# Earlier expert loads into reordered slots, a shorter router gap, and token rows gathered by DMA for experts 1 to 7

## The reference

```
def moe_swiglu(v, router, wg, wu, wd):
    logits = (v @ router).astype(F32)
    top_val, top_idx = lax.top_k(logits, TOP_K_EXPERTS)       # 2 of 8
    top_w = jax.nn.softmax(top_val, axis=-1)
    combine = jnp.sum(jax.nn.one_hot(top_idx, N_EXPERTS, dtype=F32) * top_w[..., None], axis=-2)
    ...
    for e in range(N_EXPERTS):
        y = y + combine[..., e:e + 1] * swiglu(v, wg[e], wu[e], wd[e])
    return y
```

## Time and profile before

| | us |
|---|---|
| median of 3 executions | 1486.5 (1485.67 to 1486.66) |
| profiled execution, its own time | 1487.51 |
| its span in the profile | 1485.8 |
| PE busy | 1453.5 (98%) |
| DVE, ACT, POOL busy | 619.3, 458.5, 39.9 |

### The profile page before, as it was taken

How to read it: one execution, slowest core, us unless ns; L and a number is a source line. 1 busy time by engine, 2 the same in 40 slices (tenths; PEclk the granted TensorE clock), 3 DMA queues, 4 the chain that set the end, 5 groups by cost and what they waited for, 6 DMA issues and landing times.

```text
span 1485.8 us, 28756 instructions
## 1 busy us (share of the span) xinstructions
PE 1453.5 (98%) x12424; PEld 1015.2 (68%) x12424; DVE 619.3 (42%) x879; ACT 458.5 (31%) x653; POOL 39.9 (3%) x73
## 2 busy tenths in 40 slices
PE   8999999999999999999999999999999999999967
PEld 7888788888888888888886743576346733576226
DVE  5877797645455677788840010101000010101024
ACT  5656444534445555653420000000000000000024
POOL 3200000000000010000000000000000000000000
PEclk9999999999999999999999999999999999999999
DMA  8355455556656544545669999999999999999980
GB/s 300 126 169 170 143 160 168 188 180 195 196 174 197 165 143 141 172 143 180 241 268 405 408 405 407 408 405 408 406 408 406 407 405 402 408 401 408 401 329 29
DMA packets 160948, 411.35 MB, mean 277 GB/s; under 512 B 16386, under 2 KB 41780, under 8 KB 160820
## 3 DMA queue, kind: packets, MB, share of 16 engines
q1 hardware_dynamic: 159168, 407.69, 74.1%
q10 hardware_dynamic: 1652, 1.80, 0.4%
HBM read 408.38 MB, written 1.05 MB: 276 GB/s over the span
## 4 chain that ended last, share of the span: by engine, by line
PE 92%; DMA 3%; SPq 2%; DVE 1%; issue 1%; ACT 0%; POOL 0%; POOLq 0%; DVEq 0%; ACTq 0%
PE ps L2044 35%; PE ps L1594 15%; PE ps L1596 15%; PE ps L1595 15%; SPq L532 2%; PE ps L2013 2%; PE ps L2036 1%; PE ps L1693 1%; DMA arena<-in_moe_wd 1%; DMA expert_ring<-in_moe_wd 1%; DMA split_area_hi<-in_moe_wd 1%; PE ps L1654 1%; PE ps L1840 1%; PE ps L1703 1%; PE ps L1864 1%
## 5 line engine op out<-in xcount | busy, mean ns | idle before, releaser
L1594 PE MATMUL ps<-whi,ahi 128*128 128x512 f32 (+1 forms) x984 | 391.7, 398 | 4.5 <-DVE wlo L994 2.3
L1596 PE MATMUL ps<-wlo,ahi 128*128 128x512 f32 (+1 forms) x984 | 383.7, 390 | 0.0
L1595 PE MATMUL ps<-whi,alo 128*128 128x512 f32 (+1 forms) x984 | 383.0, 389 | 0.0
L994 DVE TENSOR_TENSOR wlo<-arena,whi 128x1024 fp32r<-128x1024 f32 (+1 forms) x246 | 289.0, 1217 | 91.4 <-ACT whi L649 90.4
L649 ACT ACTIVATE whi<-arena 128x1024 fp32r<-128x1024 f32 (+1 forms) x246 | 245.7, 1053 | 97.1 <-PE ps L1596 89.2
L2044 PE MATMUL ps<-arena 128*32 128x512 f32 (+3 forms) x2724 | 224.8, 471 | 8.3 <-DMA arena<-in_moe_wu 8.3
L1594 PEld LDWEIGHTS ps<-whi,ahi 128*128 128x128 f32 x984 | 185.1, 188 | 47.4 <-issue 9.0
L1596 PEld LDWEIGHTS ps<-wlo,ahi 128*128 128x128 f32 x984 | 184.9, 188 | 39.0
L1595 PEld LDWEIGHTS ps<-whi,alo 128*128 128x128 f32 x984 | 185.4, 188 | 35.6
L2044 PEld LDWEIGHTS ps<-arena 128*32 128x32 f32 x2724 | 115.7, 110 | 103.2 <-issue 57.9
L1511 DVE TENSOR_TENSOR ff_area<-ff_area,ps 128x768 f32<-128x768 f32 (+1 forms) x24 | 19.7, 821 | 388.4 <-PE ps L2044 388.4
(11 more groups left out here) (263 smaller groups left out, 1014.8 us busy)
## 6 DMA issues: line engine op xcount, KB each, us to landing
arena<-in_w_in SPq DMA_DIRECT2D x112, 512.0 KB, 4.5
arena<-in_moe_wd SPq DMA_DIRECT2D x92, 512.0 KB, 12.5
arena<-in_moe_wu SPq DMA_DIRECT2D x78, 512.0 KB, 13.3
arena<-in_moe_wg SPq DMA_DIRECT2D x68, 512.0 KB, 13.6
expert_ring<-in_moe_wd SPq DMA_DIRECT2D x52, 512.0 KB, 12.3
expert_ring<-in_moe_wg SPq DMA_DIRECT2D x46, 512.0 KB, 13.3
expert_ring<-in_moe_wu SPq DMA_DIRECT2D x34, 512.0 KB, 14.4
arena<-in_moe_wg SPq DMA_DIRECT2D x42, 384.0 KB, 12.5
```

What stands on the lines that cost most here:

```text
L994: return V.tensor_tensor(dst, src, hi.bitcast(f32), ALU.subtract)
L1594: TE.matmul(o, ahi[:, sa], whi[:, sw], start=start, stop=False)
L1595: TE.matmul(o, alo[:, sa], whi[:, sw], start=False, stop=False)
L1596: return TE.matmul(o, ahi[:, sa], wlo[:, sw], start=False, stop=stop)
```

## The change

The diff has three parts.

1. **Slots.** The place `turned_v` in `EXTRA`, which waited for the router, becomes `states`: the same columns of `arena`, but free once a mixer step is done (`pe_step`), since the turned activations (`VT`) move to other columns. `FREED` is reordered, each slot waits for its own last user (slots 5 and 6 wait for `acc_out_dve` and `merged_ready`, not for `aT_ready`), and granules 0 and 1 of the experts are issued between the loads of `w_out` (`EARLY`).
2. **Router gap.** The second row of throw-away transposes has 3 in place of 16. The tokens of expert 0 are gathered by 16 float32 products from `u_nat`, as those of the others were, in place of 32 split ones. The low parts on DVE are gone.
3. **Rows.** POOL stores the normed activations to a DRAM buffer of 1 MB. For each of experts 1 to 7 PE works out which token is in which slot (two products with one column, `tokens_of_slots`), DVE casts that to integers, POOL issues an indirect DMA that gathers 64 or 96 rows of 4 KB into `wk(YM, ...)`, and PE transposes them (`turn_rows`, 4 transposes for each half) in place of the 8 products for each half.

```
-EXTRA = ("keys", "split_hi", "split_lo", "turned_v")
+EXTRA = ("keys", "states", "split_hi", "split_lo")
...
-FREED = [FIRST_EXTRA + i for i in range(3)] + [4, 5, 6]
-for last in range(M0 - RAW, M0):
-    FREED += [last % RAW] + (pair_of(last % WR) if last >= M0 - WR else [])
-FREED.insert(8, FIRST_EXTRA + 3)
+FREED = [FIRST_EXTRA + i for i in range(len(EXTRA))] + [5, 6, 4]
+FREED += [last % RAW for last in range(M0 - RAW, M0)]
+for last in range(M0 - WR, M0):
+    FREED += pair_of(last % WR)
+EARLY = {M0 - 4: 0, M0 - 3: 1}
...
+            def gather_rows():
+                for t in range(NT):
+                    pool.wait_ge(v_nat, t + 1)
+                    pool.dma_start(v_dram[t * P:(t + 1) * P, :], u_nat(t)).then_inc(v_stored, 16)
+                pool.wait_ge(v_stored, 16 * NT)
+                for e in range(1, NE):
+                    pool.wait_ge(slots_ready, e)
+                    if e > 1:
+                        pool.wait_ge(combined, NT * (e - 1))
+                    pool.indirect_dma_start(out=wk(YM, D)[0:CAPS[e]], out_offset=None, in_=v_dram[:, :],
+                                            in_offset=bass.IndirectOffsetOnAxis(ap=token_of[0:CAPS[e], e:e + 1], axis=0))\
+                        .then_inc(tokens_landed, 16)
...
                             if kind == "down" and j == 3:
+                                if e + 1 < NE:
+                                    dve.wait_ge(slots_done, e + 1)
+                                    V.tensor_copy(token_of[:, e + 1:e + 2], bank(7, 1, 500)).then_inc(slots_ready, 1)
...
-                    keep_busy(16, 0)
+                    keep_busy(3, 0)
...
+                    def tokens_of_slots():
+                        for t in range(NT):
+                            last = TE.matmul(bank(7, 1, 500), psel[:, t * P:(t + 1) * P].bitcast(f32), token_ids[:, t:t + 1],
+                                             start=t == 0, stop=t == NT - 1)
+                        last.then_inc(slots_done, 1)
+                    def turn_rows(e, half):
+                        n = CAPS[e]
+                        for c in range(4):
+                            last = TE.transpose(bank(7, n, c * n), wk(YM + (4 * half + c) * P, P)[0:n], ident[0:n, 0:n])
+                        last.then_inc(gathered, 1)
...
                             if j in (6, 7) and e + 1 < NE:
                                 if j == 6:
-                                    pe.wait_ge(onehot, 2 * e + 4)
+                                    pe.wait_ge(tokens_landed, 16 * (e + 1))
                                     pe.wait_ge(turned_out, e + 1)
...
-                                gather_rank(e + 1, j - 6)
+                                turn_rows(e + 1, j - 6)
```

More of the change, by code:

```diff
@@ L152, in raw @@
                     return arena[:, T + 1024:T + 1024 + GRAN]
-                if where == "turned_v":
+                if where == "states":
                     return arena[:, T + 3072:T + 3072 + GRAN]
@@ L487, in split, with fetch @@
                 sp.wait_ge(lo_ready, 2 * (n + 1))
+            of_place = [0]
+            def fetch(m):
+                slot = SLOT_OF[m]
+                if BEFORE[m] is not None:
+                    sp.wait_ge(gemm_done, M0 + BEFORE[m] + 1)
+                elif slot >= FIRST_EXTRA:
+                    if EXTRA[slot - FIRST_EXTRA] == "keys":
+                        sp.wait_ge(hg_x, 8 * DEPTH)
+                    elif EXTRA[slot - FIRST_EXTRA] == "states":
+                        sp.wait_ge(pe_step, N_STEPS + 32)
+                    else:
+                        sp.wait_ge(gemm_done, L1 + G_BR + 4)
+                elif slot >= ARENA_SLOTS:
+                    ring = (slot - ARENA_SLOTS) % WR
+                    sp.wait_ge(gemm_done, max(n for n in range(M0) if n % WR == ring) + 1)
+                elif slot < RAW:
+                    split(max(n for n in range(M0) if n % RAW == slot))
+                elif slot == 4:
+                    sp.wait_ge(at_ready, 4 * 6)
+                elif slot == 5:
+                    sp.wait_ge(acc_out_dve, upto(DVE_OUT, 1, A_BR + 4))
+                else:
+                    sp.wait_ge(merged_ready, 4)
+                for src, how, w in moe_granule(of_place[m // PER_E], m % PER_E) if m < N_MOE else granule(1, G_PLE0 + m - N_MOE):
+                    sp.dma_start(place(slot, how, w), src).then_inc(moe_landed[slot], 16)
             for n in range(M0):
@@ L513, in _ @@
                     of_place += [sp.value_load(order[0:1, RANK[e]:RANK[e] + 1], min_val=0, max_val=NE - 1) for e in range(1, NE)]
[L514 to L532, removed]
+                fetch(m)
             sp.wait_ge(gemm_done, M0 + N_MOE)
@@ L2117, in transpose_ff @@
                         last.then_inc(m_tr, 1)
-                    pe.wait_ge(v_lo, NT)
+                    pe.wait_ge(v_nat, NT)
+                    pe.wait_ge(onehot, 2)
                     for half in range(2):
-                        gather(half, onehot, 2, gathered)
+                        gather_rank(0, half, 6 + half)
                     for e in range(NE):
@@ L2153, in _ @@
                                 transpose_ff(e, PAIRS - 1, j - 6)
+                            if j == 2 and e + 1 < NE:
+                                pe.wait_ge(onehot, 2 * e + 4)
+                                if e > 0:
+                                    pe.wait_ge(slots_ready, e)
+                                tokens_of_slots()
                             if j == 4:
```

69 lines of the change are left out of this document (32 added, 37 removed).

## The result

The changed kernel takes 1497.8 us (median of 1494.3, 1497.8 and 1498.7) against 1486.5; the ratio is 1.0066, with a 95% interval of 1.0053 to 1.0080. That ratio makes 9.8 us (7.9 to 11.9) of the 1486.5, where +1.4 was forecast, and outside the range of 1481.5 to 1493. It is not the quotient of the two medians, which lie 11.3 us apart; in all that follows, differences of time go by such ratios. The profiled execution took 1494.3 us with a span of 1492.5, so the trace is that of the fastest of the three. The kernel is still one stream of DMAs with a tail, and most rows look as forecast. As in the rows of before, a row of windows has the stretch and its length, then busy us (instructions) of PE, PEld, DVE, ACT and POOL, the granted clock of PE, the share of the DMA engines, and GB/s.

The account below looks back on a forecast made before the run. One stream of expert-weight DMAs at full rate plus a 44.5 us tail bounds the kernel. Profiled 1487.5 us, -3.4 for lead, +4.8 for rows, gives 1488.9; the median is 1.0 lower: 1487.9 us, range 1481.5 to 1493.

Parts of the forecast that it names:

- What bounds the kernel: From 762 us on: one stream of weight DMAs at full rate, then a tail of 44.5 us the change leaves alone.
- The slots: Before the experts: no pause at 750 to 762 us, 17 granules issued by 757 us, slots full at about 768.
- PE's start: Behind the router: gather starts 2.5 us earlier at about 765.6 and, slowed 1.45 us by the clock, ends 1.05 earlier.
- slower by the clock: Rival: PE at 1.2 GHz through gather and first granule, experts start 1.5 us later; 1491.4 us, chance 0.10.
- The lead at granule 34: In expert 0: old backlog of 5.8 us plus 0.5 from PE's earlier start, so the stream is 6.3 us ahead.
- The pause at the table reads: At 822 to 828 us: SP's seven reads leave the engines dry for 5.5 - 2.58 = 2.9 us.
- The lead kept: Behind the table reads: 6.3 - 2.9 = 3.4 us, kept to the end.
- PE's 14.5 us: In experts 1 to 7: PE work saved by transposes in place of gather products, worth nothing at the end.
- The rows: In the experts' stream: 480 gathered rows of 4 KB, 1.97 MB, priced by bytes at 4.8 us.
- The upper bound, 9.7: High bound in us for the cost of the gathered rows: twice their bytes.
- slower by the rows: Rival: rows fetched singly through POOL's descriptors cost twice their bytes, 9.7 us; 1492.8 us, chance 0.14.
- The gathers were never late: In experts 1 to 7: rows asked for 17 us ahead in the shortest case; PE's waiting for them costed at nothing.

Follow-up runs that it names:

- e1: The change's slots and router gap only, tokens of experts 1 to 7 gathered by PE products as before, no indirect DMAs; 1483.2 us, ratio 0.9979.
- e9: Changed kernel with a plain DMA of 64 rows on POOL's queue, onto every second partition, for each indirect one; 1489.1 us, ratio 1.0010.
- e11: The change's slots and router gap, all gathers on PE, SP's table reads moved ahead of granule 17; 1485.1 us, ratio 0.9980.
- e13: Changed kernel with a plain DMA of 64 rows on POOL's queue, onto partitions 0 to 63, for each indirect one; 1493.8 us, ratio 1.0036.
- e2: Changed kernel without its seven indirect DMAs, turning and other waits kept, wrong tokens for experts 1 to 7; 1483.7 us, ratio 0.9985.
- e12: Changed kernel with only SP's table reads moved ahead of granule 17; 1494.2 us, ratio 1.0043.
- e14: Changed kernel without its indirect DMAs and with SP's table reads moved ahead of granule 17; 1482.1 us, ratio 0.9968.
- e4: The changed kernel measured again, nothing altered; 1495.3 us, ratio 1.0067.
- e7: Changed kernel with a plain DMA of the first 64 or 96 rows on POOL's queue for each indirect one; 1495.0 us, ratio 1.0049.
- e8: Changed kernel with a plain DMA of 64 or 96 rows on ACT's hardware queue for each indirect one; 1496.4 us, ratio 1.0055.

## Why the prediction was wrong, step by step

- **What bounds the kernel: right.** One stream, an end set by its last landing, a tail of 43.9 us (44.5 before).
- **The slots: right.** No pause at 750 to 762 us, 17 granules issued by 756.1 us (757), dry at 770 (768). The two early granules held nothing back.
- **PE's start: right in size (first product 2.7 us earlier, 1.2 without the offset, forecast 1.05), with the clock's loss in another place.** The forecast had the lower level last until 768.5 and slow the gather by 1.45 us. In this trace it lasted as long (6.8 us) but from 757.8 to 764.6, and fell on the second half of the router's products and the 14 transposes. First before, then after:

```profile
759.02 1.95 PE L1976 MATMUL ps<-router,arena 128*128 128x8 f32 x16 [0.61 <-ACT arena L855]
```
```profile
757.52 3.35 PE L2008 MATMUL ps<-router,arena 128*128 128x8 f32 x16 [0.61 <-ACT arena L890]
758.00:762.00 4.00, 4.00 (x20) 4.00 (x20) 0.92 (x8) 2.69 (x4) 1.72 (x3) 0.50 1.03 410
```

So the counts ended 1.6 us later than before, without the offset, and from there to the first product it was 4.33 us in place of 7.18. That `psel` was ready at 765.45 (765.1) and the gather began at 765.60 (765.6) is luck: the offset and the clock's loss, 1.5 and 1.6 us, cancel. In the traces with a low stretch of 10.2 us (e1, e9, e11, e13) nothing of PE's gain was left: from the last issue of `w_branch` to the first product of the experts it was 80.0 us, as in before (79.9), where the changed kernel has 78.7. That is part of what the rival "slower by the clock" named, which had PE start 1.5 us later than before.
- **The lead at granule 34: right.** It was issued at 818.09, 2.0 us earlier, 0.5 without the offset, as forecast, and landed in 4.5 us (median of its two halves, 9.8 in the earlier trace rows, 4.0 forecast). Its last half landed at 823.5 in place of 831.2: 7.7 us, 6.2 without the offset, forecast 6.3.
- **The pause at the table reads: right in place, too small in size.** Granule 35 landed 3.0 us earlier than before (830.8 against 833.8), 1.5 without the offset: of 6.2 us the pause took 4.7, and not 2.9. "5.5 - 2.58" counts from issue to issue. But between the landings of 34 and 35 there are 7.3 us, and 7.3 - 2.6 = 4.7: the issues lay 5.8 us apart, and granule 35 landed 6.9 us behind its issue where 34 took 5.4, which is lost too. Why 35 took longer no run shows. Most of it is there without any gather (6.8 us between the same two landings in e2). The lead kept was 1.2 us by the stream's bytes at 172 MB, not 3.4. Reading early gave 2.2 (e12) to 3.1 us (e14) back and not all 4.7. There the stream runs below its full rate with PE busy throughout, 351 to 372 GB/s from 816 to 834 us, so it seems to go at PE's pace.
- **PE's 14.5 us: right for this kernel**, which did not get faster by them (e2, with them, is no faster than e1). Four transposes take 0.46 us, for which 0.6 was forecast; the two of the earlier trace rows that this came from are 128 columns wide, not as narrow as a gather's. In a kernel without the pause they may be worth something: e14 keeps a lead that e11 loses, with the reserve on these two traces above.
- **The rows: the step that failed.** "480 rows by bytes, 4.8 us", since "the rows have the length of those of the weights, so by bytes is the nearest price". They cost 9.9 us, twice that, in this trace and again in e4. Nothing was wrong with the count of rows, their bytes or their packets; the price of a packet was (218 ns, where the stream's take 163), and that of the stream's beside it. e13 against e9 shows that 64 rows together cost 2.8 times as much as the same rows spread. The upper bound, 9.7, nearly came out as the value, which is luck, for another reason than the rival "slower by the rows" had: e7 and e8 fetch neighbouring rows by plain DMAs, e8 from ACT's queue without POOL, and cost nearly the same.
- **The gathers were never late: right.** In the experts PE's waits for DMAs are all for weights, none for rows. The five largest groups have 30.3 us, those of before 14.8 in four. The largest of before, then the two largest of after (us, times, longest):

```profile
PE ps L2044 <- DMA arena<-in_moe_wu: 8.3, 2, 8.2
```
```profile
PE ps L2081 <- DMA arena<-in_moe_wu: 11.6, 7, 8.2
PE ps L2081 <- DMA arena<-in_moe_wd: 6.8, 10, 1.1
```

Sum by the trace: -1.2 + 9.9 - 0.4 (tail and rounding) = +8.3 against the forecast of -3.4 + 4.8 = +1.4. Of the 6.9 us between them, 5.1 are the rows and 2.2 the lead, less the 0.4. The ratio gives 9.8, whose interval begins at 7.9.

**Open.** The traces of the changed kernel, here and in e4, are of its fastest execution; its medians are 3.5 and 1.65 us above them. What its other executions lose beside the six steps no trace shows, so the 9.9 us may be a little less than what the rows cost in the median. e1 is 3.1 us faster than before by its runs, while its trace has a lead of 0.9 us at 172 MB. Its profiled execution (1486.9) was 3.6 above its median, with TensorE low for 10.2 us behind the router, where the trace of before has 6.8; how much of the 3.1 is lead, I can't divide. In the traces with the new filling SP's last loads come another microsecond late (at 406 MB); the end did not show it, and I did not follow it up. Which unit the neighbouring partitions share stays open too, since no trace here names the engine of a packet. Indirect rows onto every second partition, and neighbouring rows elsewhere than from partition 0 on, weren't tried.

## What to carry to other kernels

A DMA put beside a saturated stream is priced by where it lands as well as by its bytes. Here rows that covered all 128 partitions, or every second one, cost their bytes, and 32 to 96 on neighbouring partitions 1.7 to 2.8 times theirs, so that 128 rows were cheaper than 64. Try those two forms before counting bytes. A lead won by filling slots early is worth only what the issuer's later pauses and the reader's pace leave of it, so look for the first pause that the old backlog hid. Before differences of a microsecond or two are read from two traces, an instruction ahead of the change must stand at the same time in both.

## What the runs showed of the hardware that was not expected

- Rows of 4 KB beside a stream at 407 GB/s, per DMA: 32 rows 0.7 us, 64 rows 1.3 to 1.8, 96 rows 1.6 to 2.0, 128 rows 1.2, 64 rows on every second partition 0.55. By bytes they would be 0.32, 0.64, 0.97, 1.29 and 0.64.
- The stream's own packets of 4 KB slow from 163 ns to 210 and 221 in the two windows shown while such a DMA runs. A share of busy DMA engines of 1.03 says nothing of the rate: 353 and 408 GB/s both stood under it.
- SP's seven reads of table entries spread over 3.9 us, between two issues 5.8 us apart (818.09 to 823.90); with nothing queued behind them, 171 GB/s were moved from 822 to 828 us in place of 408.
- Of the 16 traces, whose kernels are the same up to there, seven have TensorE at its lower level for 3.4 us near the start, two for 6.8 us and seven not at all. SP's last issue of `w_branch` came at 690.4 to 690.7 us without it, at 692.1 to 692.7 with 3.4 us, and at 693.6 and 693.9 with 6.8.
